# Down projection: 17 of 22 k-pairs in seven products, seven third sums in DRAM, DVE's sums ahead of piece a

## The reference

```python
h = rms_norm(x, attn_norm)
p = h @ w_in                      # 2048 x 5376, split into attention and HGRN2 parts
x = x + concat(attention, hgrn2) @ w_out          # 2048 x 2048
h = rms_norm(x, ffn_norm)
u = h @ w_up                      # 2048 x 11264
u = sum(conv_w[j] * pad(u)[j:j + S] for j in range(3)) + conv_b
a, b = split(u, 2)
return x + (silu(a) * b) @ w_down # 5632 x 2048
```

## Time and profile before

| | |
|---|---|
| median of 3 runs | 1080.2 us (1080.14 to 1080.43) |
| the profiled execution | 1080.29 us, span 1078.6 us |
| PE busy | 1073.7 us, 100% of the span |
| DVE busy | 908.6 us, 84% |
| ACT busy | 633.9 us, 59% |
| POOL busy | 79.8 us, 7% |
| moved by DMA | 260.8 MB, mean 242 GB/s |
| down projection on PE | from 857.2 us |

### The profile page before, as it was taken

How to read it: one execution, slowest core, us unless ns; L and a number is a source line. 1 busy time by engine, 2 the same in 40 slices (tenths; PEclk the granted TensorE clock), 3 DMA queues, 4 the chain that set the end, 5 groups by cost and what they waited for, 6 DMA issues and landing times.

```text
span 1078.6 us, 18188 instructions
## 1 busy us (share of the span) xinstructions
PE 1073.7 (100%) x6543; PEld 928.9 (86%) x6543; DVE 908.6 (84%) x1376; ACT 633.9 (59%) x930; POOL 79.8 (7%) x114
## 2 busy tenths in 40 slices
PE   9999999999999999999999999999999999999998
PEld 9888888888888889888888988888888888888887
DVE  7878988889655678888888888888877889999997
ACT  7677676757554655545555555545555566656663
POOL 4500000000000000000000000000000000000000
PEclk9999999999999999999999999999999999999999
DMA  8656687777889888798888888889888789798884
GB/s 275 183 163 176 190 229 223 216 223 222 234 258 245 278 236 235 240 256 239 249 232 243 237 255 245 227 258 247 271 240 235 218 282 319 256 309 315 260 289 163
DMA packets 192336, 260.77 MB, mean 242 GB/s; under 512 B 9605, under 2 KB 143894, under 8 KB 192022
## 3 DMA queue, kind: packets, MB, share of 16 engines
q1 hardware_dynamic: 176246, 216.24, 62.4%
q0 software_dynamic: 13344, 38.80, 17.6%
q10 hardware_dynamic: 2688, 5.00, 1.2%
HBM read 255.02 MB, written 43.78 MB: 277 GB/s over the span
## 4 chain that ended last, share of the span: by engine, by line
PE 99%; DMA 1%; DVE 0%; SPq 0%; issue 0%; DVEq 0%
PE bank L1821 38%; PE bank L1829 20%; PE bank L2216 7%; PE bank L2215 7%; PE bank L2214 7%; PE bank L2067 3%; PE bank L1868 3%; PE bank L2068 3%; PE bank L2069 3%; PE bank L1869 3%; PE bank L1870 3%; PE bank L1789 1%; PE bank L1897 1%; DMA xt<-in_x_dram 1%; PE bank L2106 0%; PE bank L1986 0%
## 5 line engine op out<-in xcount | busy, mean ns | idle before, releaser
L792 ACT CAST w_hi<-raw 128x1024 fp32r<-128x1024 f32 x299 | 311.9, 1048 | 252.7 <-PE bank L1829 118.4
L1201 DVE TENSOR_TENSOR w_lo<-raw,w_hi 128x1024 fp32r<-128x1024 f32 x299 | 363.8, 1222 | 108.1 <-ACT w_hi L792 107.5
L1821 PE MATMUL bank<-hs,w_hi 128*128 128x512 f32 x1792 | 423.0, 391 | 0.0
L1821 PEld LDWEIGHTS bank<-hs,w_hi 128*128 128x128 f32 x1792 | 331.3, 188 | 66.2 <-issue 0.9
L1829 PEld LDWEIGHTS bank<-hs,w_lo 128*128 128x128 f32 x1792 | 224.6, 192 | 5.7 <-issue 0.2
L1829 PE MATMUL bank<-hs,w_lo 128*128 128x256 f32 x1792 | 227.3, 283 | 0.0
L1171 ACT CAST hi_slot<-slot 128x1024 fp32r<-128x1024 f32 (+1 forms) x102 | 117.7, 1187 | 64.7 <-DVE slot L1746 25.2
L1728 DVE TENSOR_TENSOR slot_lo<-slot,hi_slot 128x1024 fp32r<-128x1024 f32 (+1 forms) x102 | 136.7, 1388 | 5.8 <-ACT hi_slot L1171 4.7
L2216 PE MATMUL bank<-hi_slot,gated 128*128 128x512 f32 (+1 forms) x194 | 75.1, 387 | 0.0
L2214 PE MATMUL bank<-hi_slot,gated 128*128 128x512 f32 (+1 forms) x194 | 75.1, 387 | 0.0
L1646 DVE SCALAR_TENSOR_TENSOR C<-U,cols,C 128x256 f32<-128x256 f32 x176 | 73.3, 478 | 0.0
(11 more groups left out here) (248 smaller groups left out, 1183.8 us busy)
## 6 DMA issues: line engine op xcount, KB each, us to landing
raw<-in_w_ffn_up_dram SPq DMA_DIRECT2D x176, 512.0 KB, 5.2
u_sums<-in_w_ffn_down_dram POOLq DMA_DIRECT2D x58, 512.0 KB, 6.7
raw<-in_w_in_dram SPq DMA_DIRECT2D x51, 512.0 KB, 4.5
slot<-in_w_ffn_down_dram SPq DMA_DIRECT2D x38, 512.0 KB, 5.0
slot<-u_sums SPq DMA_DIRECT2D x74, 256.0 KB, 5.6
raw<-in_w_in_dram SPq DMA_DIRECT2D x66, 256.0 KB, 4.2
raw<-in_w_out_dram SPq DMA_DIRECT2D x32, 512.0 KB, 5.7
u_sums<-u_sums POOLq DMA_DIRECT2D x16, 512.0 KB, 7.4
```

Source lines behind the costliest of these rows:

```text
L792: act.copy(w_hi[:, i, :], raw[:, i, :]).then_inc(units_hi, 1)
L1201: dve.tensor_tensor(w_lo[:, i, :], raw[:, i, :], w_hi[:, i, :].bitcast(F32), ALU.subtract)\
L1821: m = pe.matmul(banks[b][:, :], w_hi[:, i, c], hs[:, 4 * i + k, :], start=(first and k == 0), stop=(final and k == 3))
```

## The change

`PATTERNS`: in each column pair one eight becomes a seven. Pair 0 had four C, eight S, D, eight S, c; it gets four C, seventeen S, c. Pair 1 had C, c, three S, D, seven S, D, six S, C, c; it gets C, c, nine S, D, eight S, C, c. SEVENS goes from 16 to 17, so one more k-pair has its activation sums made and parked (three parked sets instead of two, in use in turns 6 to 8 instead of 5 and 6). Seven third sums are made in DRAM instead of five, which with the extra k-pair makes 82 POOL steps instead of 74. They begin at unit 18 instead of 20, follow each other by 3 units instead of 3.5, and pause three times (units 30 to 38, 97 to 101, 127 to 135) instead of once. The region shared by parked sums and x2 grows by 768 bytes a partition, and small constants are put into common tiles. In pair 1 the parked sums are fetched behind k-pair position 6 instead of 7; all four x2 parts now wait for the parked sets. In `lo_of`, DVE makes sums 3 and 4 ahead of the split of piece a instead of behind it; the wait for sum 4 stays ahead of the split of b.

```diff
--- before.py
+++ after.py
@@ -79,15 +79,15 @@
 Q_DOWN = Q_UP + 2 * UP_GROUPS
 QUADRUPLES = KT_FF // 2
 COLUMN_PAIRS = OUT_GROUPS // 2
-PATTERNS = ["CCCCSSSSSSSSDSSSSSSSSc", "CcSSSDSSSSSSSDSSSSSSCc"]
+PATTERNS = ["CCCCSSSSSSSSSSSSSSSSSc", "CcSSSSSSSSSDSSSSSSSSCc"]
 KINDS = "".join(PATTERNS)
 SEVENS = PATTERNS[0].count("S")
 SEVEN_AT = [[at for at, kind in enumerate(pattern) if kind == "S"] for pattern in PATTERNS]
 EIGHT_AT = [[at for at, kind in enumerate(pattern) if kind != "S"] for pattern in PATTERNS]
 RESIDENT_SUMS = 14
 PARKED_SUMS = SEVENS - RESIDENT_SUMS
-THIRD_SUM_IN_DRAM = (1, 4, 7, 10, 13)
-LAST_PARKED_TURN = 6
+THIRD_SUM_IN_DRAM = (1, 3, 15, 5, 8, 11, 13)
+LAST_PARKED_TURN = 8
 FIRST_PARKED_TURN = LAST_PARKED_TURN - PARKED_SUMS + 1
 SEVEN_ORDER = [*range(FIRST_PARKED_TURN), *range(RESIDENT_SUMS, SEVENS), *range(FIRST_PARKED_TURN, RESIDENT_SUMS)]
 K_PAIR_AT = [[SEVEN_ORDER[SEVEN_AT[pair].index(at)] if at in SEVEN_AT[pair] else SEVENS + EIGHT_AT[pair].index(at)
@@ -113,8 +113,8 @@
 
 SLOT_OF = slots_in_turn()
 HI_SLOTS = 2
-SUM_STEP = (7, 2)
-FIRST_SUM_UNIT, SUM_PAUSE = 20, (30, 38)
+SUM_STEP = (3, 1)
+FIRST_SUM_UNIT, SUM_PAUSES = 18, [(30, 38), (97, 101), (127, 135)]
 SCRATCH = 1024
 
 G_OUT = 0
@@ -158,21 +158,19 @@
         consts_start = nc.sbuf_base
         neg_sink = sb("neg_sink", [P, HEADS])
         sink = sb("sink", [P, HEADS])
-        eps = sb("eps", [P, 1])
         N_SMALL = 2 * HG_HEADS + 3 + 2 * KT
         N_CONV = 2 * D_FF // P
-        cols = sb("cols", [P, N_SMALL + (1 + CONV) * N_CONV])
+        N_COLS = N_SMALL + (1 + CONV) * N_CONV
+        cols = sb("cols", [P, N_COLS + 2 + TT])
+        eps, qk_gain, q_eps = cols[:, N_COLS:N_COLS + 1], cols[:, N_COLS + 1:N_COLS + 2], cols[:, N_COLS + 2:N_COLS + 2 + TT]
+        norms = sb("norms", [P, 4 * TT])
+        ss, neg_ss, o_ss = norms[:, 0:TT], norms[:, TT:2 * TT], norms[:, 2 * TT:4 * TT]
         lb = sb("lb", [P, HG_HEADS])
         one_lb = sb("one_lb", [P, HG_HEADS])
         lb_t = sb("lb_t", [P, 4, HG_HEADS])
-        qk_gain = sb("qk_gain", [P, 1])
-        q_eps = sb("q_eps", [P, TT])
         q_scale = sb("q_scale", [P, 2, TT, 2])
-        ss = sb("ss", [P, TT])
         ss_part = sb("ss_part", [P, TT, OUT_GROUPS])
         x_rms_row = sb("x_rms_row", [P, SEQ])
-        neg_ss = sb("neg_ss", [P, TT])
-        o_ss = sb("o_ss", [P, TT * 2])
         partial_of_p7 = nc.alloc_sbuf_tensor_at("partial_of_p7", [P, GT], F32, offset=consts_start)[:, :]
         assert consts_start + GT * 4 <= nc.sbuf_base
         X_GAIN = [0, KT]
@@ -208,7 +206,7 @@
         all_mean = sb_at(place, "all_mean", [P, P])
         rows = sb_at(place, "rows", [P, 1 + 1 + CONV, P])
 
-        small = region("small_region", 8448)
+        small = region("small_region", 9216)
         place = list(small)
 
 
@@ -534,8 +532,8 @@
 
         X2_PARTS = [(1, 1), (1, 0), (0, 0), (0, 1)]
         X2_PARTS_APART = 2 - (PARKED_SUMS - 1)
-        SUMS_BACK_AT = [5, 7]
-        X2_BACK_AT = [[5, 14, 17, 20], [13, 15, 17, 19]]
+        SUMS_BACK_AT = [5, 6]
+        X2_BACK_AT = [[15, 17, 19, 20], [14, 16, 18, 19]]
         FIRST_HALF, SECOND_HALF = slice(0, GT // 2), slice(GT // 2, GT)
 
         def last_half(pair):
@@ -748,8 +746,9 @@
 
             def wait_for_step(step):
                 unit = FIRST_SUM_UNIT + step * SUM_STEP[0] // SUM_STEP[1]
-                if unit >= SUM_PAUSE[0]:
-                    unit += SUM_PAUSE[1] - SUM_PAUSE[0]
+                for pause in SUM_PAUSES:
+                    if unit >= pause[0]:
+                        unit += pause[1] - pause[0]
                 pool.wait_ge(units_used, unit + RING)
 
             def column_block(tile, c):
@@ -1305,7 +1304,7 @@
             dve.memset(dist[first, CHUNK:P], FAR).then_inc(dist_made, 1)
             dve.wait_ge(rows_transposed, 2)
             dve.tensor_copy(cols[:, KT:N_SMALL], bank_rows[:, KT:N_SMALL])
-            dve.tensor_copy(cols[:, N_SMALL:], bank_rows[:, N_SMALL:N_SMALL + (1 + CONV) * N_CONV])\
+            dve.tensor_copy(cols[:, N_SMALL:N_COLS], bank_rows[:, N_SMALL:N_SMALL + (1 + CONV) * N_CONV])\
                 .then_inc(cols_made, 1)
             make_lo(1, 1)
             dve.wait_ge(x_squared, 2 * TT)
@@ -1748,9 +1747,10 @@
             def lo_of(pair, at):
 
                 q = q_of(pair, at)
+                if is_seven(pair, at):
+                    sums_of_weights(pair, at)
                 for piece in pieces_of(q):
                     if piece == "b" and is_seven(pair, at):
-                        sums_of_weights(pair, at)
                         dve.wait_ge(sums_of_block_made, seven_of(pair, at) + 1)
                     split(q, piece)
                     if (q, piece) == ADDED_BEHIND:
```

## The result

The changed kernel took 1081.69 us (median of 18 runs, 1080.77 to 1085.1); the kernel before, beside it on the same chip, 1080.19 us (18 runs, 1079.95 to 1080.79). The ratio is 1.0016, interval 1.0009 to 1.0023: slower, though within the 0.2% that the prediction calls the same. The forecast was 1079.5 us, the range ended at 1081.6. Six matmuls less were to bring 1.36 us, and the time went up by 1.5.

A forecast was written before the change was run, and what follows sets the result against it. PE was taken as the bound, a row of matmuls without a hole, with DVE close ahead in the down projection. 1080.2 - 1.36 for six matmuls + 0.7 of holes = 1079.5 us, range 1078.6 to 1081.6.

The forecast's parts named there:

- The matmuls: Down projection, one eight made a seven per column pair: six matmuls of 0.2267 us fewer, 1.36 us less.
- The pace of DVE: New order saves 0.12 us per seven: 5.15 us from sum to sum for a plain seven, 4.54 with DRAM third sum.
- Pair 0: First column pair, down projection: the lead runs out, holes at q16, q17, q19 of 0.6 us, taken as 0.7.
- lead: Time between the end of DVE's split of piece b and PE's need; k-pairs of both column pairs count q0 to q43.
- the prediction's own bound: No hole in the first column pair if third sums come 0.7 us sooner; lead starts at 2.3, ends near 0.1.
- Pair 1: no hole: Second column pair, down projection: lead near 1.9 us at q24, about 0.9 at the ninth seven, then refilled; no hole.
- Costed at nothing: the fetch of the parked sums: 1152 KB in place of 768, used some 19 us later: no cost; uncovered, its transfer, 7 to 8 us, once.
- the bound of 1.64 us: Most lead a seven with third sum from DRAM can have, given 5.74 us from its place coming free to use.
- Rival A: Third sums come sooner, so no hole opens on PE in the down projection; 1078.85 us, chance 0.22.
- Rival B: DVE's new order earns nothing, holes of 2.0 us in the first column pair; 1080.8 us, chance 0.18.
- Rival C: Denser POOL accumulations hold up weight loads before the down projection; 1082.8 us, chance 0.12.

The follow-up runs named there:

- nine third sums in time: Changed kernel with order by kind, nine third sums in DRAM, POOL's second and third pauses left out, fetch in one piece: 1080.64 us, 1.0006.
- order by kind: Changed kernel, sums ahead of the split of a only where DVE computes the third sum, behind it where that comes from DRAM: 1081.16 us, 1.0005.
- the one with the moved step: Changed kernel with POOL's second pause at units 83 to 89 in place of 97 to 101: 1081.93 us, 1.0016.
- the steps alone: Kernel before with only POOL's new pacing (first unit 18, every 3 units, three pauses), still 74 steps: 1080.58 us, 0.9999.
- the small fetch: Changed kernel with only one of three parked sets (384 KB) fetched in pair 1, values of two k-pairs wrong: 1080.81 us, 1.0002.

## Why the prediction was wrong

**The matmuls.** Right: six less, and the 0.2267 us step holds between holes. PE's time in the down projection is -1.36 and +2.23 of new holes (0.86 and 1.37), which makes the +0.87.

**The pace of DVE.** Right to 0.01 us: 5.14 and 4.54. The Trainium skill (VectorE: DVE Perf Modes, The DRAIN you can't avoid) says of a semaphore after each operation, from a test with eight copies, that it costs nothing extra; the runs show 0.72 us from start to start where the split waits for sum 4 (old order) and 0.60 where it doesn't (new order), so for these operations the measurement decides against it.

**Pair 0.** Right in mechanism and place, and in size partly by luck. Forecast 0.6 to 0.7 us of holes at q16, q17 and q19; measured 0.86 new, at q14, q16, q17 and q19. The first lead, q7, is 2.3 where 1.66 stood, since its third sum came at 888.84, not at 889.4; from q8 on (1.93, 1.36, 0.98, 1.20, 0.82, 0.43) plain sevens lose 0.39 and DRAM ones win 0.22 as the working has it, but q9 lost 0.57, its third sum being awaited for 0.69 us. By the prediction's own bound a lead that starts at 2.3 leaves no hole; two things that it lacked made up for the better start. One is q9's late sum. The other is what PE needs: the prediction opened a hole where the lead fell below 0 and took 0.1 us each for three waits, but in these profiles a hole opens where the lead falls below about 0.2, and closes back to 0.2. The leads at q14, q16, q17 and q19 were 0.05, 0.03, -0.18 and 0.02, the holes 0.15, 0.18, 0.37 and 0.17: each hole and its lead add up to about 0.2. With nine third sums in time and the fetch in one piece the lead in pair 0 stays at 0.5 us and above, and pair 0 has no new hole; this bears the mechanism out.

**"Pair 1: no hole" and "Costed at nothing: the fetch of the parked sums".** This is the step that failed. I gave the transfer a cover from its own user's side (used 19 us later) and wrote that behind it "stand loads of later slots". One of those loads is the third sum of q29, which is needed as soon as it can come. I even had its price, 5.74 us from issue to use, as a term of the bound of 1.64 us, and let that price stand behind a transfer of 1152 KB. There it was 7.84 us, in the other kernels with the one piece behind 6 up to 8.68, and in one (order by kind) less, 6.90 from issue to landing. The new order makes this the moment for which the whole of DVE waits. At q28 the lead is 0.95; with q29's third sum in time it would be 0.95 + 0.22 = 1.17 at q29 and 0.78 at q30. The 1.8 us by which sum 4 starts later (999.51, where the splits ahead of it end at 997.7) turns this into a hole of 0.85 at q29, and the plain sevens behind it, q30 and q32, add 0.37 and 0.15, until the D. The "7 to 8 us, once" that the prediction put down for an uncovered transfer was not the price either: it took 8.8 us, and what it cost was the lateness of a small load behind it, less the lead. Three pieces instead of one bring back 1.6 us, a third of the bytes 1.3 (against their own before: 1.0001 and 1.0002, where the changed kernel has 1.0016); one piece at position 4, 6 or 7 gives 1.0012, 1.0016, 1.0019.

The order isn't what makes it: with the old one the sum of q29 is as late (8.68 us), DVE comes to it with a lead of 0.64 at q28 in place of 0.95, and pair 1 loses 1.74 us. With the order by kind, which has both savings, the lead at q28 was 1.63 in the profiled execution, and the hole stayed shut. Split a as cover and 0.12 us more in each seven are worth about the same here.

**The rest, left open.** The profiled execution is accounted for: 1080.29 - 1.36 + 2.23 of new holes + 0.09 ahead of the down projection is 1081.25, measured 1081.22. The median of the timed runs is 0.5 us above it and the slowest 3.9, and those executions left no trace. The profiled ones show three things that vary: the new holes of pair 1, 1.4 to 1.9 us in the changed kernel's two executions and the one with the moved step (those of pair 0 stay at 0.9); the gap at 275 us, up to 1.4 us above the normal, which differs even between two executions of the changed kernel (0.3 and 0.7); and the set-up, after which PE stands 0.4 to 0.5 us later than in before in order by kind and in the steps alone, and 2.2 us in the small fetch. Why q27's third sum varies is open, and so is why the timed runs of kernels with one large fetch spread up to 1085, while those of the kernel before stay within 0.9 us in the first comparison (in a later group they reach 1082.76); with three pieces they still spread by 2.7 us (1079.3 to 1082.0).

**Rival A** (no hole) fell at q14. (The Trainium skill, DMA: Bandwidth & Descriptors, Anatomy of one DMA, gives the formula named beside it for DMAs issued from GpSimd; these loads are issued by SP.) **Rival B** (the order earns nothing, 1080.8) was wrong in its reason and right that nothing is earned as a whole: the 0.12 is there, and the idle time for third sums takes it back. Its 2.0 us of holes come near the measured 2.23 by luck, as it put them all into pair 0. **Rival C** fell: the steps alone, 0.9999. Its deadline exists at 293 units and costs 5 us there.

**The range** was built for a pair 0 that could be mis-sized both ways, and gave pair 1 and the spread of the runs nothing above rival B's 0.8. It ended 0.1 us short of the median. Said in hindsight: with the fetch as a rival (the 1.37 us measured in pair 1: 1079.5 + 1.4 = 1080.9 us) and the same 0.8 above it, the range would have ended at 1081.7 and just held the median.

## What to carry to other kernels

For every transfer that is enlarged or moved, list what is queued behind it until the queue next runs empty, and compare each one's issue-to-use time with the lead of its user; that its own user comes late is only half of its cover. Try a large transfer that isn't urgent in pieces, between the small urgent ones. Try an operation that waits for a DMA behind everything that doesn't need it: here, putting it first to save a semaphore wait paid only where the DMA was already there. And take the arrival of a load as a range, not as the one time that a trace shows: a lead that is to hold must cover its late end.

## What the runs showed of the hardware

- A 256 KB load from DRAM into a slot landed 4.8 to 6.8 us after its issue in this loaded queue (third sums of the changed kernel's first profile from q7 on, without q29's). With 1152 KB issued 5.2 us ahead on the same queue, q29's landed after 7.7 to 8.6 us in six profiles and after 6.9 in one. Three pieces of 384 KB at three places left it at 5.1 to 6.1 us. The Trainium skill (DMA: Bandwidth & Descriptors, Rules for kernel authors) asks for 1 MiB or more in a DMA for bandwidth and for small ones to be made into a large one; for the same bytes, three of 384 KB at three places were 1.6 us better here than one of 1152. The rate at the place, about 400 GB/s with one and 310 to 410 with three, was high either way, so no bandwidth was gained; that the order of arrival is what counted is read from this, and not tested by itself.
- Of two DVE operations on 128x512 f32, the second starts 0.60 us after the first without a wait between them and 0.72 us with one, though a row shows each as 0.68.
- A hole on PE is under-told by its own row: a hole of 0.39 us (0.62 between starts) shows as 0.23 us idle, and most of 2.23 us of holes only in the rows of the weight loads (3.2 us, nine times).
- PE's products with a piece come without a hole only where DVE's split of it has ended about 0.2 us ahead of them: in the changed kernel a hole and the lead at it add up to 0.19 to 0.21 us at q14, q16, q17 and q19.
- A gap of 0.7 to 1.7 us (normal 0.3) at the entry of the output projection, with no releaser, in some executions and not in others, and once so and once not in the same kernel. Its cause is open.
